# Leaving out key blocks of two steep ALiBi heads in a hybrid attention kernel, with a norm check on the chip and a second complete program behind it

## The reference, cut to what matters

```python
h = rms_norm(x, g_pre);  proj = h @ w_in            # (S, 5648), split into all that follows
# mixer A: 4 heads, two q/k maps of width 64 per head, value width 128
scale = 64 ** -0.5;  slopes = 2 ** (-8 * (1..4) / 4)       # 1/4, 1/16, 1/64, 1/256
s = q @ k.T * scale - slope * (qpos - kpos)          # causal, for each map
p = softmax(s);  o = (p[map 0] - lam * p[map 1]) @ v
oa = rms_norm(o, g_sub_a) * (1 - lam_init);  ya = (oa * silu(za)) @ w_up_a
# mixer B: gated linear attention, 4 heads, state carried along the sequence
yb = (rms_norm(gla(q_b, k_b, v_b, decay), g_sub_b) * silu(zb)) @ w_up_b
y = sigmoid(gate_a) * ya + sigmoid(gate_b) * yb
out = x + rms_norm(y @ w_out, g_post)
```

## Time and profile before

| | |
|---|---|
| median of 3 runs | 1437.21 us |
| profiled execution, span of its slowest core (core 2) | 1450.2 us |
| spans of the 8 cores in it | 1423.1 to 1450.2 us |
| die medians in it | 1438.6 us at clock 0.984, 1429.6 us at 0.993 |
| TensorE busy | 1361.1 us (94%) |
| ScalarE busy | 848.3 us (58%) |
| VectorE busy | 772.7 us (53%) |
| GpSimd busy | 198.7 us (14%) |

### The profile page before, as it was taken

One profiled execution on the slowest core, in us unless ns is written; L12 is line 12 of the kernel. 1 busy time (PEld: TensorE's weight loads), 2 busy tenths in 40 slices (PEclk: granted clock), 3 DMA queues, 4 the chain that ended last, 5 costly groups with the idle time before them and its releaser, 6 DMA issues.

```text
span 1450.2 us, 31152 instructions; the slowest of 8 cores (1423.1 to 1450.2 us)
## 1 busy us (share of the span) xinstructions
PE 1361.1 (94%) x11086; PEld 764.5 (53%) x11280; DVE 772.7 (53%) x2273; ACT 848.3 (58%) x1168; POOL 198.7 (14%) x303
## 2 busy tenths in 40 slices
PE   4998999899999999999999999999999999999996
PEld 2344445444555554655555555566555666655632
DVE  4569657664765455654647335464354643234744
ACT  4346437433664466645775667756678667778612
POOL 1024102110211021100201002011011110000100
PEclk9887889999999999999999999999999999999999
DMA  9998798223543344232433225323234212214143
GB/s 263 303 239 231 208 277 266 102 70 135 189 161 115 120 155 165 92 143 89 178 143 117 88 88 184 137 89 111 84 134 168 88 59 89 88 63 172 41 153 127
DMA packets 54279, 207.54 MB, mean 143 GB/s; under 512 B 6880, under 2 KB 15472, under 8 KB 39152
## 3 DMA queue, kind: packets, MB, share of 16 engines
q1 hardware_dynamic: 54128, 205.54, 42.8%
HBM read 173.01 MB, written 32.51 MB: 142 GB/s over the span
## 4 chain that ended last, share of the span: by engine, by line
PE 84%; DMA 4%; DVE 4%; issue 4%; ACT 3%; SPq 1%; POOL 0%; DVEq 0%; ACTq 0%; POOLq 0%
PE ps_pg L491 57%; PE ps_acc L491 16%; PE ps_qk L811 9%; DMA sb_wbuf<-wsc 2%; PE ps_pg L495 2%; ACT sb_PT L819 1%; DMA sb_KT<-w_in 1%; DMA sb_KT<-w_up_a 1%; ACT sb_tmp L647 0%; DVE sb_xr L939 0%; DVE sb_cum L705 0%; SPq L561 0%; DVE sb_szB L648 0%; DMA sb_xr<-x 0%; DVE sb_gatedB L782 0%
## 5 line engine op out<-in xcount | busy, mean ns | idle before, releaser
L819 ACT ACTIVATE sb_PT<-ps_qk 128x1024 bf16<-128x1024 f32 (+1 forms) x544 | 519.0, 997 | 225.7 <-PE ps_qk L811 218.8
L491 PE MATMUL ps_pg<-sb_hT,sb_wbuf 128*128 128x512 bf16 x1583 | 429.8, 388 | 11.1 <-DVE sb_wbuf L568 2.9
L491 PE MATMUL ps_acc<-sb_V,sb_PT 128*128 128x129 bf16 x4224 | 427.9, 221 | 11.8 <-ACT sb_PT L819 4.8
L491 PEld LDWEIGHTS ps_acc<-sb_V,sb_PT 128*128 128x128 bf16 x4224 | 313.9, 98 | 147.4 <-issue 45.9
L491 PE MATMUL ps_pg<-sb_wbuf,sb_hT 128*128 128x512 bf16 x906 | 239.6, 388 | 11.2 <-DVE sb_statE L861 1.8
L491 PEld LDWEIGHTS ps_pg<-sb_hT,sb_wbuf 128*128 128x128 bf16 x1664 | 155.3, 99 | 157.6 <-issue 53.6
L909 DVE SCALAR_TENSOR_TENSOR sb_tmp<-sb_tmp,ps_pg 128x512 f32<-128x512 f32 x128 | 87.8, 687 | 221.0 <-PE ps_acc L491 143.8
L811 PE MATMUL ps_qk<-sb_QT,sb_KT 64*128 64x256 bf16 (+1 forms) x2176 | 163.8, 270 | 5.9 <-ACT sb_PT L819 3.1
L894 ACT ACTIVATE sb_tmp<-ps_pg 128x512 f32<-128x512 f32 x128 | 76.5, 597 | 118.0 <-PE ps_pg L491 85.2
L491 PEld LDWEIGHTS ps_pg<-sb_wbuf,sb_hT 128*128 128x128 bf16 x960 | 88.7, 99 | 95.6 <-issue 34.8
L863 POOL TENSOR_TENSOR sb_statE<-sb_statE,sb_mhalf 128x1 f32<-128x1 f32 x128 | 74.4, 588 | 372.7 <-DVE sb_statE L861 362.9
(11 more groups left out here) (136 smaller groups left out, 1308.4 us busy)
## 6 DMA issues: line engine op xcount, KB each, us to landing
sb_wbuf<-wsc SPq DMA_DIRECT2D x100, 1024.0 KB, 5.1
sb_KT<-w_in SPq DMA_DIRECT2D x88, 256.0 KB, 8.8
sb_xr<-x SPq DMA_DIRECT2D x36, 512.0 KB, 4.8
out<-sb_xr SPq DMA_DIRECT2D x32, 512.0 KB, 3.2
sb_xa<-x SPq DMA_DIRECT2D x28, 512.0 KB, 5.9
wsc<-sb_wbuf SPq DMA_DIRECT2D x9, 1024.0 KB, 9.5
wsc<-sb_V SPq DMA_DIRECT2D x6, 1024.0 KB, 9.6
sb_KT<-w_out SPq DMA_DIRECT2D x16, 256.0 KB, 8.0
```

Of the source, the lines that this page charges most:

```text
L491: return P.op(_pe(n), lambda e: e.matmul(out=out_f(), lhsT=lf(), rhs=rf(), start=start, stop=stop, **kw), reads=reads, writes=writes, mode ...
L819: P.op({"act": (0.075 + width / 600.0, 0.1)}, lambda e: e.activation(out=PT[pt.i][:, :, 0:width], in_=qk[:, 2 * half:2 * half + 2, 0:width ...
```

## The change

The file keeps all its stages. The builder is put into a function `program(tag, near)` that plans a complete kernel with its own semaphores. It is called twice: with `near=True` for the program that always runs, and with `near=False` for a complete second one, the same as before, that runs only if a flag is not zero. With `near=True`:

- A key block is left out where it is more than `REACH[h]` blocks of 128 away from the query block. `REACH` comes out as 5, 18, 70 and 277 blocks, against at most 31 blocks that exist, so heads 2 and 3 lose nothing. Pairs with no live block go; a pair with live blocks in part has fewer matmuls and a narrower exp.
- Each tile gets `norms(t)`: squares of Q and K of heads 0 and 1 (two instructions over 1024 elements, on VectorE or ScalarE), four matmuls of 512 columns in 32-column tiling of the array, and one maximum on VectorE.
- After the last of them `decide` brings the maximum together into `flag` (four small VectorE instructions, one matmul of one column), and every engine gets one wait for it.
- At the end of its instructions every engine reads `flag` into a register and branches over the second program if it is zero.

```diff
+NORM_LIMIT = 134.0
+REACH = [int((104.0 + 2 * 137.0 / 8 + 127 * s) / (128 * s)) for s in SLOPES]
...
+            def norms(t):
+                P.at(t, t + 1, "norm")
+                for key, dst, src, deps in (("sqq", junk, QT[t % 2][:, 0:2, :], [f"QT{t % 2}_{h}" for h in range(2)]),
+                                            ("sqk", sqk, KT[:, 0:2, t * T:(t + 1) * T], [f"KT{h}_{t}" for h in range(2)])):
+                    keys = ["junk0", "junk1"] if key == "sqq" else ["sqk"]
+                    P.op({"dve": _dve(1024, 1.0), "act": _act(1024)}, ...square of src into dst..., reads=deps, writes=keys)
+                b = P.buf("pg")
+                for j in range(4):
+                    P.op({"pe": (0.004 if j else 512 / 2400.0 + 0.1, 0.17)}, lambda e, j=j, b=b: e.matmul(
+                        out=pg[b.i][32 * j:32 * j + 32, :], lhsT=block2[:, j // 2, :], rhs=(junk, sqk)[j // 2][:, j % 2, :], start=True, stop=True,
+                        tile_position=(0, 32 * j)), ..., writes=[b], mode="col32", atom=("norm", t))
+                P.op({"dve": _dve(512)}, lambda e, b=b: e.tensor_reduce(out=norm[:, t:t + 1], in_=pg[b.i][:, :], axis=AX.X, op=ALU.max),
+                     reads=[b], writes=[f"norm{t}"])
+
+            def decide(t):
...
+                small("dve", 1, lambda e: e.tensor_scalar(out=okay[:], in0=norm[:, NT:NT + 1], scalar1=NORM_LIMIT, scalar2=None, op0=ALU.is_le),
+                      ["normx"], ["okay"])
+                b = P.buf("pg")
+                mm(lambda b=b: pg[b.i][:, 0:1], ones[:], okay[:], True, True, 1, ["ones", "okay"], [b])
...
+                P.op({"sp": (0.05, 0.0)}, lambda e: None, reads=["flag"], writes=["flagsp"])
+                for en in ("pe", "act", "dve", "pool"):
+                    P.op({en: (0.05, 0.0)}, lambda e: None, reads=["flag"], writes=[f"flag{en}"])
...
         def stage_batt(t, ws):
...
+                if near:
+                    keep = P.stream
+                    norms(t)
+                    if t == ntiles - 1:
+                        decide(t)
+                    P.stream = keep
...
-            pairs = [(h, u, i) for h, u in units for i in range(2 * t + u + 1)]
+                def live(h, u, i, kbi, a):
+                    d = 2 * (2 * t + u - i) + a - kbi
+                    return d >= 0 and (not near or d <= REACH[h])
...
+                pairs = [(h, u, i) for h, u in units for i in range(2 * t + u + 1) if pieces(h, u, i)[0]]
...
-            nb = len(pairs) // 2
-            for b in range(nb + 1):
-                if b < nb:
-                    atom = (t, b)
-                    qk_pair(pairs[2 * b], 0, atom, pairs[2 * b + 1])
-                    qk_pair(pairs[2 * b + 1], 1, atom)
+                duos = [pairs[i:i + 2] for i in range(0, len(pairs), 2)]
+                for b in range(len(duos) + 1):
+                    if b < len(duos):
+                        for i, p in enumerate(duos[b]):
+                            qk_pair(p, i, (t, b), duos[b][1] if i == 0 and len(duos[b]) == 2 else None)
...
+        first, quick = program("n", True)
+        rest, full = program("f", False)
...
+        def run(name):
+            def body(e):
+                quick[name](e)
+                far = e.value_load(flag[0:1, 0:1])
+                with e.If(far != 0):
+                    e.drain()
+                    e.sem_inc(gate, 1)
+                    e.wait_ge(gate, len(ENGS))
+                    full[name](e)
+
+            return body
```

More of the change, by code:

```diff
@@ L329, in make @@
             return body
-        for eng_name, deco in block_engines.items():
-            deco(make(eng_name))
+        return {eng_name: make(eng_name) for eng_name in ENGS}
 def _pe(n):
@@ L439, in _build @@
         stg = [KT[:, i // 2, 2048 + (i % 2) * 1024:2048 + (i % 2 + 1) * 1024].bitcast(F32) for i in range(NSTG)]
+        sqk = SB("sqk", [128, 2, T], BF16)
+        block2 = SB("block2", [128, 2, 32], BF16)
+        ones = SB("ones", [128, 128], BF16)
+        norm = SB("norm", [128, NT + 2], F32)
+        okay = SB("okay", [128, 1], BF16)
+        flag = SB("flag", [128, 1], mybir.dt.int32)
         qk = PSM("qk", [128, 4, 512], F32)
@@ L457, in _build @@
[L457 to L461, removed]
-        block = es.enter_context(nc.Block())
[L464 to L496, removed]
@@ L499, in _build @@
[L499 to L519, removed]
-        small("pool", 4, lambda e: e.memset(mhalf[:], -0.5), [], ["mhalf"])
-        small("pool", 256, lambda e: e.memset(state[:], 0.0), [], ["state"])
@@ L523, in _build @@
-        small("pool", 128, lambda e: e.memset(stbf[:], 0.0), [], ["stbf"])
-        small("pool", 1024, lambda e: e.memset(qtT[:], 0.0), [], ["qtT0", "qtT1"])
-        def v_ef(half):
-            for par in range(2):
-                vv = V[:, half * 2 * NT:(half + 1) * 2 * NT, :, 128].rearrange("p (g two) h -> p g two h", two=2)[:, :, par, :]
-                small("dve", 64, lambda e, vv=vv, par=par: e.tensor_copy(out=vv, in_=eft[:, par * 4:par * 4 + 4].unsqueeze(1).to_broadcast([128, NT, 4])),
-                      ["eft"], [f"Vef{half}{par}"] + (["vxdone"] if half else []))
@@ L601, in group @@
-        def group(b, n, reads, lhs, rhs, count=512, claim=(), after=(), out_f=None, last=(), mode="full"):
-            for kc in range(n):
-                mm(out_f or (lambda: pg[b.i][:, :]), lambda kc=kc: lhs(kc), lambda kc=kc: rhs(kc), kc == 0, kc == n - 1, count,
-                   reads if kc in (0, n - 1) else [], [b] + (list(last) if kc == n - 1 else []), mode=mode, claim=claim if kc == 0 else (),
-                   after=after if kc == 0 else ())
-        def wk(w):
-            return [(w, k) for k in range(8)]
@@ L611, in fm @@
-        def fm(w, t, col, b, claim=(), after=(), last=()):
-            group(b, 8, wk(w) + [f"hT{t % 2}_{s}" for s in range(4)], lambda kc: wbuf[w.i][:, kc * 512 + col:kc * 512 + col + 128],
-                  lambda kc: hT[t % 2][:, kc, :], claim=claim, after=after, last=last)
-        def tm(w, t, s, b, claim=(), after=()):
-            group(b, 8, wk(w) + [f"hT{t % 2}_{s}"], lambda kc: hT[t % 2][:, kc, s * 128:(s + 1) * 128],
-                  lambda kc: wbuf[w.i][:, kc * 512:(kc + 1) * 512], claim=claim, after=after)
@@ L651, in b_qa @@
-        def b_qa(w, t):
-            for j in range(4):
-                b = P.buf("pg")
-                fm(w, t, j * 128, b, after=[f"QT{t % 2}_{j}"])
-                copy(lambda j=j: QT[t % 2][:, j, :], lambda b=b: pg[b.i][:], [b], [f"QT{t % 2}_{j}"], 512)
-        def b_ka(w, t):
-            for j in range(4):
-                b = P.buf("pg")
-                fm(w, t, j * 128, b)
-                copy(lambda j=j: KT[:, j, t * T:(t + 1) * T], lambda b=b: pg[b.i][:], [b], [f"KT{j}_{t}"] + (["stgdone"] if t == 4 else []), 512)
@@ L978, in _build @@
+        for name, deco in (("pe", block.tensor), ("act", block.scalar), ("dve", block.vector), ("pool", block.gpsimd), ("sp", block.sync)):
+            deco(run(name))
         _build.sbuf_left = nc.sbuf_bytes_remaining
```

904 lines of the change are left out of this document (509 added, 395 removed).

## The result

The changed kernel is faster, but by less than forecast: ratio 0.9656 (95% interval 0.9579 to 0.9732), with runs of 1396.29 and 1381.86 us against 1437.2. Timed again as the first experiment, beside more runs of the kernel before, it is 0.9648 (0.9622 to 0.9675). That is 50 us saved where 73 were forecast, and some 1388 us where the range ended at 1386. (Two more of its four runs took 1579.95 and 1588.14 us, with one die at a granted clock of about 0.81 to 0.83 throughout; such runs are left out of every comparison.) The profiled execution took 1396.29 us with a span of 1394.3.

What follows compares the result with a forecast made beforehand. Outside the start, TensorE's issue time was taken as the bound. -83.0 + 3.3 + 1.5 + 3 + 2 = -73 us, taking 1437.21 to 1364 us (chance 0.77); its own range 1354 to 1386, 8 in 10 from 1346 to 1386.

Steps and rivals of the forecast that it cites:

- work removed: Attention on TensorE: 49.8 us of matmuls into acc, 23.6 of QK columns, 9.6 of changeovers; 83.0 us saved.
- norm matmuls: Each tile's four 512-column matmuls on TensorE run side by side: 3.3 us in all, 8.6 if one after another.
- rest of the checks: Squares and maxima in the first 200 us and the held pg tile: 1.5 us, bounds 0 and 5.6.
- second program: At the end, SyncE's flag read and far jump: 3 us, bounds 0 and 6.4; other engines' jumps off the path.
- the seam: End of the last tile: second mixer's dependent steps have less attention work between them; 2 us, bounds 0 and 8.
- The step that failed: Outside the start, time is TensorE's issue time, so each instruction removed from it gives back its pace; 83.0 us.
- the signs named beforehand: Profile after: expected counts, TensorE 93 to 95% busy, tile 7 over 25 us shorter; wrong if tiles 5-7 idle more.
- rival A: Half the freed time given back, as second mixer's dependent steps or ScalarE set the pace: 1403 us, chance 0.12.
- B: TensorE's 17.7 us of waits before acc and QK go too, nothing charged at the last tile's end: 1344 us, chance 0.09.
- C: On some core the flag isn't zero and the complete second program runs after the first: 2801 us, chance 0.02.

Runs made afterwards that it cites:

- the first experiment: The changed kernel timed once more with no edit, against the kernel before: ratio 0.9648 (0.9622 to 0.9675).
- the cut alone: Key blocks left out as in the changed kernel, but no norms, decision or second program; against the kernel before: ratio 0.9551.
- plan 2: Planner's modelled latency between engines 0.17 instead of 0.15 us: kernel before with all its work, ratio 1.0069; with only the key blocks cut, 0.9552.
- the better plan: Whole change with SyncE's jump before its last wait, modelled latency 0.18, and norms, decay stream and attention shifted in the plan; against the kernel before: ratio 0.9482.
- the cut in place: Kernel before in its own instruction order, with instructions of dead key blocks struck out after planning; against the kernel before: ratio 0.9796.
- the run with tile 7 full: Key blocks cut without checks or second program, but tile 7 keeps all its key blocks; against the kernel before: ratio 0.9695.
- the checks alone: Kernel before with all key blocks, plus norms and decision, without second program; against the kernel before: ratio 1.0078.

## Why the prediction was wrong

The terms of the sum, against the account (us; the change as timed again):

| term | forecast | measured |
|---|---|---|
| work removed | -83.0 | -83.6 |
| norm matmuls | 3.3 | 3.2 |
| rest of the checks | 1.5 | 5.6 |
| second program | 3 | 7.3 (6.6 by the times) |
| gaps of the cut in its new plan (forecast: the seam) | 2 | 17.8 |
| sum | -73 | -50 |

**The removed work was right.** 49.8 us into acc were forecast and 50.0 found in the cut alone; 23.6 and 24.6 for QK, 9.6 and 9.0 for changeovers. As the account sets the pace by the columns, this mostly confirms the counts. That the time was really TensorE's is shown by tiles 3 to 6: in the cut alone they are 46 us shorter, where 51 were forecast, with 1.4 us more of gaps.

**The norm matmuls were right.** They run side by side, as the QK couples do. Core 2 in tile 5:

```profile
784.62 0.39 PE L700 MATMUL ps_pg<-sb_junk,sb_block 128*32 128x512 bf16 x2
784.62 0.39 PE L700 MATMUL ps_pg<-sb_sqk,sb_block 128*32 128x512 bf16 x2
784.95 0.56 PE L880 MATMUL ps_qk<-sb_QT,sb_KT 64*128 64x256 bf16 x8
```

All four start within 10 ns and the next atom starts 0.33 us later. With changeovers they are 3.2 us (1.8 + 1.4) for the 3.3 forecast. The Trainium skill's rule of parallel tiles (TensorEngine Tiling (Array Packing), Key Properties) holds here, and the loss of fast weight load that the same page warns of could not be seen: a 32-column load is shown as 92 ns, a 128-column one as 98. The squares are cheaper on VectorE than forecast, 689 ns where twice 698 were charged:

```profile
L696 ACT ACTIVATE sb_junk<-sb_QT 128x1024 bf16<-128x1024 bf16 x5 | 5.3, 1057 | 8.6 <-PE ps_pg L700 8.3
L697 DVE TENSOR_TENSOR sb_sqk<-sb_KT 128x1024 bf16<-128x1024 bf16 x5 | 3.4, 689 | 0.2 <-ACT sb_KT L490 0.2
```

**The step that failed** is the one from "TensorE waits for little" to "an instruction taken from it should give back its pace", outside the start and the seam. The prediction charged 2 us for uncovered waits, all at the end of tile 7, and nothing in any other tile, and it had no term for the new order that the planner writes. Measured are 18 us for the cut alone, in tiles 1, 2 and 7. The argument behind the step was that TensorE hardly waits before acc and QK and is busy for 96 to 98%. Both rows are true and say nothing on this: they show that the waits were covered, not what covered them. The wait rows of the other stages (ScalarE's and VectorE's groups, each behind TensorE) would have been the ones to price. Two things stand behind the 18 us.

Cover: in an unchanged order the cut uncovers 41 us of waits, and the new plan has 23 us less. At the seam, 5 to 6 us are left in three plans and go when the blocks are put back. That is more than the 2 charged but within the bound of 8; some 2 of it are matmuls at 1.2 GHz, for which the sum had no term. In tile 2, 2 to 3 us are of this kind.

The plan as a term of its own: with equal work another order alone moved the time by 10 us. It makes 3 to 4 us in tile 2, about 5 of the 9 us of the checks, and whatever in tile 1 is not chance. With plan 2 on both sides the cut had no more gaps than the full work, so how much of the 18 us belongs to the cut in general stays open.

**Of the signs named beforehand,** the counts (445, 3340, 1754) and the norms' start times came true. TensorE's busy share is 92%, not 93 to 95; tile 7 is 18 us shorter on core 6, not over 25; tile 1 ends later; and TensorE's idle time in tile 7 grew, which was named as a sign of being wrong.

**The second program** was forecast at 3 us and cost 6.6 by the times. Rows of the changed kernel on core 2, the flag's load and the branch on each engine's queue (duration min/median/max, start):

```profile
L1055 SPq TENSOR_LOAD <-sb_flag x1: 469/469/469, 1391.1 to 1391.1; - x1
...
L1056 PEldq COMPARE_BRANCH  x1: 4743/4743/4743, 1380.7 to 1380.7; - x1
...
L1056 SPq COMPARE_BRANCH  x1: 50/50/50, 1391.6 to 1391.6; - x1
```

SyncE's next instruction stands at 1394.04, 2.4 us behind the end of this branch. Load, branch and that pause are 3.0 us, as forecast. The pause agrees with the stall that the Trainium skill has for a taken branch to a far target (Runtime: NRT & Kernel Launch, Instruction fetch mechanics); that it is a fetch, the trace does not show. On TensorE the time, 4.7 us, is inside the branch; it is hidden. Beside these 3.0 us the landing of the last output grew from 2.7 to 3.4 us. Why it grew is open. Some 2.8 us of the 6.6 lie elsewhere, in an order that is the same as without the second program, and are not explained.

**The rivals.** The time came out between the forecast and rival A, which had the dependent steps of the second mixer set the pace. That is what tile 7 shows, but it is 5 to 6 us and not half of the removed work; the rest of the miss is the plan, the checks and the second program. B (more than the bare pace) did not come. C did not either: no instruction of the second program ran. That the time missed the range by only 2 us is luck: the gaps of the cut (17.8) and the second program (6.6) lie beyond their bounds (8 and 6.4), and the norm matmuls (3.2) stayed far under the 8.6 that the end of the range had for them.

## What to carry to other kernels

A saturated engine's removed work comes back in full only where something else can move into its place. Before pricing a cut of the independent work, ask which dependent steps it was standing over, tile by tile, the last above all, and charge there; striking the work out of the unchanged order shows that cover directly. Where a planner writes the order, time one or two plans of equal work first: their spread (10 us here) is the least error of any forecast, and another plan after the cut was worth as much here as what the cut had lost. Before per-tile numbers of several cores are put together, look at each core's granted clock and for missing records, and see how far two profiles of one order agree.

## What the runs showed of the hardware that was not expected

A VectorE square of 128 x 1024 bf16 took 689 ns, as long as an f32 operation of 512 elements in the same kernel (698 ns). A compare-and-branch over the second program was recorded at 50 ns on SyncE with 2.4 us of silence behind it, and at 4.7 us on TensorE.

At the seam of the last tile, TensorE's granted clock fell to 1.2 GHz for 3.4 to 10.2 us on all 8 cores in each profile of a plan made for the cut, save the better plan, and on no core of the kernel before, its plan 2, the cut in place or the run with tile 7 full; with the checks alone two cores had 3.4 us. Removing work there cost clock besides waits.
